# One store of 128 partitions in place of four stores of 32 for each unit of expert results

## The reference, cut to what matters

```python
D_MODEL = 1024
N_EXPERTS = 64
TOP_K = 2
D_FF_EXPERT = 512

def hierarchical_moe(x, w_group, b_group, w_router, b_router, w1, w3, w2):
    # choice of a group of experts, then of two experts in it: expert_ids, weights
    ...
    def expert_block(args):
        xb, e = args
        return (jax.nn.silu(xb @ w1[e]) * (xb @ w3[e])) @ w2[e]
    ...
    y_sorted = yb.reshape(-1, d)[dest] * sorted_w[:, None].astype(x.dtype)
    y = jnp.zeros((t, d), x.dtype).at[sorted_tok].add(y_sorted)

def reference(...):
    h = h + hybrid_mixer(...)
    h = h + hierarchical_moe(rmsnorm(h, g_ffn[l]), ...)
    return rmsnorm(h, g_final)
```

## Time and profile before

| what | value |
|---|---|
| median of 3 runs | 2168.52 us (2167.18 to 2169.27) |
| the profiled execution, its own time | 2165.52 us |
| its span, first to last instruction | 2163.4 us |
| PE busy | 1792.8 us, 83% |
| PE weight loads (PEld) busy | 974.2 us, 45% |
| DVE, ACT, POOL busy | 484.9, 245.2, 245.7 us |
| data moved by DMA | 510.98 MB in 128219 packets |
| stores of unit results (L1328) | 400 transfers of 32 KB |
| gathers of tokens (L720) | 101 |

### The profile page before, as it was taken

The page is one execution under the profiler, slowest core; times in us unless marked ns, Lnnn a source line. Parts: engine busy times, 40 slices in busy tenths (PEclk is TensorE's granted clock), DMA queues, the critical chain, the costliest instruction groups (busy, mean ns, idle before and its releaser), DMA issues.

```text
span 2163.4 us, 39592 instructions
## 1 busy us (share of the span) xinstructions
PE 1792.8 (83%) x13826; PEld 974.2 (45%) x13827; DVE 484.9 (22%) x1147; ACT 245.2 (11%) x544; POOL 245.7 (11%) x375
## 2 busy tenths in 40 slices
PE   6999999999999999999847566777777776776574
PEld 3576556644444444445534233444444443443342
DVE  5618223421101110135631001011101111111015
ACT  4011313300000000011100000000000000000002
POOL 1951000000000000001111001111111111111013
PEclk9999999999999999999969778899989998888787
DMA  6320312101111110045469999999999999999997
GB/s 196 146 62 10 142 49 64 49 20 44 44 44 44 44 42 3 38 181 211 173 256 424 427 421 409 395 380 368 409 407 408 410 404 418 412 410 413 415 398 262
DMA packets 128219, 510.98 MB, mean 236 GB/s; under 512 B 34402, under 2 KB 84066, under 8 KB 103074
## 3 DMA queue, kind: packets, MB, share of 16 engines
q1 hardware_dynamic: 97520, 461.36, 54.2%
q0 software_dynamic: 8816, 27.02, 3.4%
q10 hardware_dynamic: 21840, 22.06, 3.0%
HBM read 479.84 MB, written 34.35 MB: 238 GB/s over the span
## 4 chain that ended last, share of the span: by engine, by line
PE 57%; DMA 33%; issue 3%; DVE 2%; ACTq 1%; ACT 1%; SPq 1%; POOLq 1%; POOL 0%; DVEq 0%
PE act_bank L766 28%; DMA gain_b<-xf_rows,gather_idx 16%; PE dve_bank L766 15%; DMA tokens<-expert_token_table 12%; PE act_bank L1095 4%; DMA unit_results<-lane_row 3%; PE dve_bank L773 2%; PE act_bank L1107 2%; DMA unit_results<-spatialT 2%; ACTq L1328 1%; PE act_bank L773 1%; PE dve_bank L1107 1%; PE dve_bank L866 1%; PE dve_bank L979 1%; PE act_bank L944 1%
## 5 line engine op out<-in xcount | busy, mean ns | idle before, releaser
L766 PE MATMUL act_bank<-norm_store,unit 128*128 128x512 f32 x1024 | 450.8, 594 | 0.2 <-DMA unit<-in_w_in 0.2
L766 PEld LDWEIGHTS act_bank<-norm_store,unit 128*128 128x128 f32 x1024 | 194.4, 190 | 240.2 <-issue 239.1
L773 PE MATMUL dve_bank<-ident,gain_b 32*128 32x32 f32 x808 | 74.2, 235 | 223.1 <-DMA gain_b<-xf_rows,gather_idx 223.1
L1107 PE MATMUL act_bank<-unit,gain_a 128*32 128x256 f32 x2432 | 203.0, 491 | 28.9 <-DVE gain_a L1849 15.3
L1095 PE MATMUL act_bank<-unit,gain_a 128*32 128x256 f32 x3200 | 194.6, 397 | 19.9 <-issue 19.1
L1847 DVE TENSOR_TENSOR gain_a<-gain_a,act_bank 128x128 f32<-128x128 f32 x100 | 28.7, 287 | 714.7 <-ACT gain_a L1316 714.7
L773 PEld LDWEIGHTS dve_bank<-ident,gain_b 32*128 32x128 f32 x808 | 64.9, 153 | 267.9 <-issue 267.9
L1095 PEld LDWEIGHTS act_bank<-unit,gain_a 128*32 128x32 f32 x3200 | 108.3, 115 | 111.4 <-issue 56.4
L1107 PEld LDWEIGHTS act_bank<-unit,gain_a 128*32 128x32 f32 x2432 | 92.4, 134 | 95.1 <-issue 73.5
L1685 DVE TENSOR_TENSOR rows_store<-dve_bank,rows_store 128x512 f32<-128x512 f32 x48 | 33.2, 692 | 431.1 <-PE dve_bank L766 431.1
L1316 ACT ACTIVATE gain_a<-act_bank 128x128 f32<-128x128 f32 x101 | 28.0, 277 | 876.6 <-PE act_bank L1095 845.7
(11 more groups left out here) (267 smaller groups left out, 1446.8 us busy)
## 6 DMA issues: line engine op xcount, KB each, us to landing
unit<-in_w SPq DMA_DIRECT2D x112, 2048.0 KB, 38.2
norm_store<-in_w SPq DMA_DIRECT2D x32, 2048.0 KB, 35.0
mid_store<-in_w SPq DMA_DIRECT2D x32, 2048.0 KB, 33.5
rows_store<-in_w SPq DMA_DIRECT2D x16, 2048.0 KB
unit<-in_w_gate SPq DMA_DIRECT2D x24, 512.0 KB, 5.2
unit<-in_w_in SPq DMA_DIRECT2D x4, 2048.0 KB, 8.8
unit_results<-unit POOLq DMA_DIRECT2D x4, 2048.0 KB, 13.4
unit_results<-lane_row ACTq DMA_DIRECT2D x200, 32.0 KB, 8.0
```

Source lines behind the costliest of these rows:

```text
L766: ins = nc.tensor.matmul(out_, stationary, moving, start=first and n == 0, stop=n == len(pairs) - 1)
L773: ins = nc.tensor.transpose(bank[:, n * rows:(n + 1) * rows], block_, ident[0:rows, 0:rows])
L1107: ins = nc.tensor.matmul(y_bank[s][z * CAP:(z + 1) * CAP, 0:DQ], hidT[:, j], w2s[s][:, j, z * DQ:(z + 1) * DQ], start=j == 0, stop=j == QU ...
```

## The change

In place of four transfers, each of which takes 32 partitions of `y_rows[s]` to one block of 256 columns of 32 rows in DRAM, ACT issues one transfer of all 128 partitions. In DRAM its rows are walked in the order z (4 blocks of columns, a step of 256 elements), t (32 rows, a step of 1024), n (256 elements in a row), so every element goes to the same place as before. `y_stored[s]` counts 16 for each unit, and the waits on ACT and POOL are set accordingly.

```diff
@@ POOL, after the last unit
             for s in range(SLOTS):
-                pool.wait_ge(per_slot["y_stored"][s], last[s] * (16 * QUARTERS) + 16 * QUARTERS)
+                pool.wait_ge(per_slot["y_stored"][s], last[s] * 16 + 16)
@@ ACT
             for s in range(SLOTS):
                 act.sem_inc(per_slot["y_drained"][s], 1)
-                act.sem_inc(per_slot["y_stored"][s], 16 * QUARTERS)
+                act.sem_inc(per_slot["y_stored"][s], 16)
@@ ACT, unit_work
-                act.wait_ge(per_slot["y_stored"][s], c * (16 * QUARTERS) + 16 * QUARTERS)
+                act.wait_ge(per_slot["y_stored"][s], c * 16 + 16)
                 nc.scalar.activation(y_rows[s], y_bank[s][:, 0:DQ], ACT.Copy).then_inc(per_slot["y_drained"][s], 1)
                 act.wait_ge(per_slot["y_drained"][s], c + 2)
                 row = in_sequence(c, row_shift - UNITS)
-                for z in range(QUARTERS):
-                    act.dma_start(y_dram[bass.ds(row * CAP, CAP), z * DQ:(z + 1) * DQ],
-                                  y_rows[s][z * CAP:(z + 1) * CAP]).then_inc(per_slot["y_stored"][s], 16)
+                act.dma_start(y_dram[bass.ds(row * CAP, CAP)].rearrange("t (z n) -> z t n", z=QUARTERS), y_rows[s]
+                              ).then_inc(per_slot["y_stored"][s], 16)
```

## The result

The changed kernel takes **2438.24 us** (median of 4 runs, 2427.91 to 2439.09) against 2167.85 us before: ratio 1.1238, 95% interval 1.1214 to 1.1262. It is 270 us slower, where 206 were forecast. The profiled execution took 2437.43 us, with a span of 2435.4 us.

What follows compares the result with a forecast made beforehand. The expert stage was taken as bound by weights for about 448 us and by units for 446, with little room between. 140 + 40 + 20 + 5 = 205 us on 2168.5 gave 2374 us, range 2250 to 2500.

Steps and rivals of the forecast that it cites:

- What bounds the kernel: Expert stage: about 448 us bound by weights and 446 us bound by units, with little room between the two.
- Step 1: The merged store: its leading count of 4 puts it on four engines, 33 packets each, landing in 23.7 us against 11.7.
- The price of a packet: Stores behind weights: each packet costs 0.57 us, the turn of a 16 KB weight packet, beside a fixed 4.9 us.
- rival A: Packets cheap, engines uneven: stores land no later, only 9% more work on four engines, at most +91, 2260 us; chance 0.14.
- The landing of a store behind weights: One merged store on four engines lands 4.9 + 33 x 0.57 = 23.7 us after issue; 4 us on an idle engine.
- Steps 2 to 4: The sum's time terms: unit-bound slot waits +140, weight-bound stretches +40 and +20, ends where DMA is not full +5.
- step 2: Unit-bound stretch: 23 slot waits each grow by 8.6 us, 55 us given back behind 14 runs of waits: +140.
- The distances of copies in a slot: Sign that the forecast is right: copies in a slot 20 to 24 us apart in place of 12.3.
- step 3: Weight-bound stretches: four engines get 9% more work, +40; nine ACT waits mostly covered by arriving weights, +20.
- Step 5: ACT: three issues per unit go, 3 x 0.47 us, but ACT waits for PE anyway; changed semaphore counts cost 0.
- Rival B: Store spread over 16 engines, 9 packets in place of 12, waits 39 us shorter: 2148 us; chance 0.09.
- Rival C: Full congestion: weights in every turn, 221 or 274, +40, and 108 for nine waits: up to 2590 us; chance 0.06.

Runs made afterwards that it cites:

- lead16: The changed kernel with a unit's store walked as 16 x 8 rows instead of 4 x 32, rows in another order: 2157.72 us, ratio to before 0.9965.
- flat16: The changed kernel with a unit's 128 rows written one behind the other, in two dimensions, rows in another order: 2157.94 us, ratio to before 0.9964.
- lead2: The changed kernel with a unit's store walked as 2 x 64 rows, rows in another order: 2601.28 us, ratio to before 1.2013.

## Why the prediction was right, and where its sum went wrong

**What bounds the kernel** held. With little room between weights and units, a slower store showed at once.

**Step 1**, how the store is spread, held: 15840 packets, as forecast for four engines, and 15640, 16240 and 17040 for leading counts of 2, 8 and 16. The Trainium skill's rule on the largest count up to 16 that divides both sides (DMA: Bandwidth & Descriptors, "Why a DMA increments its semaphore by 16 and not by 1") agrees with all four.

**The price of a packet** held: 0.57 us forecast, 0.54 and 0.56 measured over whole stalls. With it falls rival A, in which several packets share a turn. The same page of the Trainium skill puts about 9 to 17 descriptors between two switches of an engine ("Queues, rings and completion order"); these runs don't agree, with 24 packets of stores between 24 of weights and 70 us for twice the packets. The landing of a store behind weights held too, forecast at 23.7 us: in the packet records nine stores found ACT's queue empty and weights streaming from their issue on, and landed 22.0 to 23.8 us after their issue. Without weights it is 3.0 us, forecast 4.

**Steps 2 to 4** took every store by itself, and there the sum failed. "4.9 + 33 x 0.57 = 23.7 us" is the landing of a store that finds the queue empty, and step 2 used it for all; 33 x 0.57 = 18.8 us of queue for a unit every 7 to 9 us doesn't leave it empty. Of the 100 stores, counted by their packets, 14 landed in 18 to 24 us, 32 later, up to 73.0, and 54 earlier, many of them in 3 us after a stall. The distances of copies in a slot, a sign that the prediction named with 20 to 24 us, say the same: of the 36 pairs 2 lie there, 10 above (up to 60.0 us) and 24 below. The waits of 461.7 us lie just over the 200 to 450 that it named; the packets (15840) and the DMA share (0.76) came out as it said. The copies, counted from the first unit, show where that told:

| part | before, us | after, us | longer by | forecast |
|---|---|---|---|---|
| start to unit 21 | to 1353.00 | to 1415.62 | 63 | steps 3, 4: under 25 |
| units 21 to 69 (unit-bound) | 1353.00 to 1799.10 | 1415.62 to 1987.07 | 125 | step 2: 140 |
| units 69 to 100 | 1799.10 to 2115.92 | 1987.07 to 2388.37 | 84 | steps 3, 4: about 40 |

That step 2 came out near its 140 is in part luck: not every wait in a slot grew by 8.6 us, but there were fewer waits (26 in the whole run) of 17.8 us each, six of them of over 40. What it gave back was too much as well: behind a wait the next copy came after 4.75 us (median) and not 1.6, and before the change after 6.4 (median of the 14) and not 5.5. The weight-bound parts were mis-sized: +147 where steps 3 and 4 gave 65. The sentence of step 3 that failed is "weights that arrive meanwhile cover most of it". A stall of over 40 us is longer than what SP has in the queue; the weights run out, and the share after it is 0.08 for 20 us. The first stall came as early as 1142.58 to 1186.70 us. Waits cover the landing only; that an issue itself could be held up, 60.1 us in all, stood in no step.

**The 9% of work on four engines** (step 3, +40 over 448 us; +91 over the whole stage in rival A) is not isolated by any run. With packets of 4 KB it is at most the 104 us by which the two kernels differ, store waits included. Its kind shows in the stall above, where four engines still move weights after the other twelve are through.

**Step 5** held as far as it goes: lead16 and flat16 differ by a quarter of a microsecond of issue per unit, beside the order of the rows, and take the same time. **Rival B**, tested by lead16, was right in kind and too large: the waits shrank by 38.6 us (39 forecast), but the kernel gained 7 us and not 20, with DMA at 404 GB/s in the unit-bound stretch and not 413. The point from which it decides (fewer than 12 packets) held, 17 packets being slower and 9 faster. **Rival C** looked for the missing time in the right place, the waits of the weight-bound parts, but its 2590 us took weights in every turn; a stall ends that by itself.

## What to carry to other kernels

Before transfers are merged, look at the first count of both sides: the merged transfer here begins with 4, and so four engines do the work of 16. For small transfers beside a stream of large packets, price the packet and not the byte, and compare packets x price for one unit of work with the time between two units; above it the transfers queue, and a landing time read from a single one no longer holds. Cutting the large packets shortens the turn, but it costs the stream its rate: 8 KB paid a little here (0.24%), 4 KB did not.

## What the runs showed of the hardware that was not expected

- An issue on ACT took 0.32 us for the form 32x256, 0.34 for 128x256, and with three dimensions 0.56 or 1.06 (four engines), 0.59 (16), 1.12 (8) in the median. Behind a long backlog an issue was held up: five in the changed kernel, for up to 16.9 us, and twelve in lead2, for up to 35.7 us.
- Two queues with work took turns on an engine packet by packet, whatever the size: 24 packets of 1 KB and 24 of 16 KB in 4 us on four engines. The same 132 packets of a store took 19.2 us beside weights and 1.8 us without.
- DMA moved 413 GB/s with weight packets of 16 KB, 407 with 8 KB and 396 with 4 KB (stretch 1799 to 2093 us, all bound by weights or nearly so).
- The chain of waits of the changed kernel puts 11% of the span down to "another core or an unknown queue", which is the wait for the stores (six pieces of 43 to 45 us). On one core a share under this name can be the kernel's own transfer.
